# Both branch outputs of a hybrid decoder layer transposed by DMA as 16-bit halves, in place of TensorE transposes

## The reference, cut to what matters

```python
h = rms_norm(x, norm_gain)
aq, ak, av, az, bqkv, bz, bbeta, balpha, gate_a, gate_b = split(h @ w_in)
ya = moba_attention(heads(aq), heads(ak), heads(av)) * silu(az)
bq, bk, bv = split(short_conv(bqkv, conv_w))
g    = -exp(a_log) * softplus(balpha + dt_bias)
beta = sigmoid(bbeta)
o  = gated_delta_rule(heads(bq), heads(bk), heads(bv), g, beta)
yb = rms_norm(o, dn_norm_gain) * silu(heads(bz))
merged = sigmoid(gate_a) * (ya @ w_branch_a) + sigmoid(gate_b) * (yb @ w_branch_b)
x = x + merged @ w_out
return rms_norm(x, final_norm_gain)
```

## Time and profile before

| what | value |
|---|---|
| time, median of 3 runs | 789.8 us |
| the profiled execution's own time | 789.82 us |
| its span | 788.1 us |
| mean granted TensorE clock | 0.997 of 2.4 GHz |
| PE busy | 777.5 us (99%) |
| DVE busy | 550.4 us (70%) |
| ACT busy | 404.6 us (51%) |
| POOL busy | 76.2 us (10%) |
| data moved by DMA | 143.09 MB, mean 182 GB/s |

### The profile page before, as it was taken

One profiled execution on the slowest core, in us unless ns is written; L12 is line 12 of the kernel. 1 busy time (PEld: TensorE's weight loads), 2 busy tenths in 40 slices (PEclk: granted clock), 3 DMA queues, 4 the chain that ended last, 5 costly groups with the idle time before them and its releaser, 6 DMA issues.

```text
span 788.1 us, 12805 instructions
## 1 busy us (share of the span) xinstructions
PE 777.5 (99%) x3651; PEld 642.8 (82%) x3651; DVE 550.4 (70%) x1265; ACT 404.6 (51%) x609; POOL 76.2 (10%) x151
## 2 busy tenths in 40 slices
PE   8999999999999999999999999999999999999996
PEld 7878888888888888888888888888888888888884
DVE  5789659956975796589569847974896466765563
ACT  5765445544554655455455445554554654345440
POOL 5110101010100100110101000001101000001120
PEclk9999999999999999999999999999999999999998
DMA  9946675665656556656756665657555566577652
GB/s 249 254 127 186 184 191 151 183 189 157 186 167 186 152 178 176 184 144 193 193 152 183 176 188 141 197 147 205 145 178 182 176 202 184 180 267 270 184 167 107
DMA packets 181161, 143.09 MB, mean 182 GB/s; under 512 B 11024, under 2 KB 146192, under 8 KB 181008
## 3 DMA queue, kind: packets, MB, share of 16 engines
q1 hardware_dynamic: 180992, 142.52, 62.7%
q10 hardware_dynamic: 144, 0.26, 0.1%
HBM read 140.64 MB, written 2.11 MB: 181 GB/s over the span
## 4 chain that ended last, share of the span: by engine, by line
PE 96%; DVE 2%; issue 1%; DMA 1%; SPq 0%; ACT 0%; POOLq 0%; POOL 0%; DVEq 0%; ACTq 0%
PE pj L551 28%; PE pj L549 28%; PE pj L550 28%; PE dn_ps L601 1%; PE pj L834 1%; PE pj L832 1%; PE pj L833 1%; DMA w_raw<-in_w_in_dram 1%; PE dn_ps L588 1%; PE dn_ps L622 0%; PE dn_ps L627 0%; DVE conv L1212 0%; PE mo_ps L657 0%; PE mo_ps L664 0%; PE dn_ps L602 0%
## 5 line engine op out<-in xcount | busy, mean ns | idle before, releaser
L1083 DVE TENSOR_TENSOR w_lo<-w_raw,w_hi 128x1024 fp32r<-128x1024 f32 x251 | 307.1, 1227 | 139.6 <-ACT w_hi L848 138.4
L549 PE MATMUL pj<-w_hi,xt_hi 128*128 128x512 f32 x860 | 346.2, 403 | 0.4 <-DVE w_lo L1083 0.4
L551 PE MATMUL pj<-w_hi,xt_lo 128*128 128x512 f32 x860 | 336.7, 391 | 0.0
L550 PE MATMUL pj<-w_lo,xt_hi 128*128 128x512 f32 x860 | 335.5, 390 | 0.0
L848 ACT ACTIVATE w_hi<-w_raw 128x1024 fp32r<-128x1024 f32 x251 | 263.4, 1056 | 132.2 <-PE pj L551 122.7
L551 PEld LDWEIGHTS pj<-w_hi,xt_lo 128*128 128x128 f32 x860 | 161.4, 188 | 34.7
L549 PEld LDWEIGHTS pj<-w_hi,xt_hi 128*128 128x128 f32 x860 | 161.7, 188 | 32.5 <-ACT gate L992 1.1
L550 PEld LDWEIGHTS pj<-w_lo,xt_hi 128*128 128x128 f32 x860 | 161.9, 188 | 30.3
L1271 DVE SCALAR_TENSOR_TENSOR xs<-lrep,xs 128x31 f32<-128x31 f32 (+30 forms) x496 | 79.9, 236 | 0.1
L1212 DVE SCALAR_TENSOR_TENSOR conv<-dn_ps,hs,conv 128x255 f32<-128x255 f32 (+2 forms) x72 | 29.4, 472 | 0.0
L484 POOL TENSOR_TENSOR xo<-v,own 128x128 f32<-128x128 f32 x16 | 7.3, 459 | 221.5 <-DVE v L1280 180.9
(11 more groups left out here) (296 smaller groups left out, 702.3 us busy)
## 6 DMA issues: line engine op xcount, KB each, us to landing
w_raw<-in_w_in_dram SPq DMA_DIRECT2D x384, 256.0 KB, 3.1
w_raw<-in_w_out_dram SPq DMA_DIRECT2D x64, 256.0 KB, 3.7
w_raw<-in_w_branch_a_dram SPq DMA_DIRECT2D x32, 256.0 KB, 3.4
w_raw<-in_w_branch_b_dram SPq DMA_DIRECT2D x32, 256.0 KB, 3.4
gate<-in_x_dram SPq DMA_DIRECT2D x8, 256.0 KB, 5.2
gate<-in_x_dram SPq DMA_DIRECT2D x4, 512.0 KB, 7.7
gate<-in_final_norm_gain_dram SPq DMA_DIRECT2D x1, 1024.0 KB, 8.9
out_dram<-gate SPq DMA_DIRECT2D x4, 256.0 KB, 3.6
```

Of the source, the lines that this page charges most:

```text
L549: pe.matmul(bank[:, t, :], hi[:, k, tok], w_hi[:, slot, cs], start=(k == 0), stop=False)
L550: pe.matmul(bank[:, t, :], hi[:, k, tok], w_lo[:, slot, cs], start=False, stop=False)
L551: mm = pe.matmul(bank[:, t, :], lo[:, k, tok], w_hi[:, slot, cs], start=False, stop=(k == kt_all - 1))
L1083: dve.tensor_tensor(w_lo[:, slot, :], w_raw[:, slot, :], w_hi[:, slot, :].bitcast(F32), ALU.subtract).then_inc(lo_ready, 1)
```

## The change

PE no longer transposes `ya` and `yb`. ACT copies each one, seen as 16-bit words, into `halves`, where the low 16 bits of all 256 words of a row (of a partition) stand first and the high 16 bits behind them. SP issues one DMA that transposes the four 128 x 128 tiles of 16-bit words from SBUF to SBUF (`halves` to `halvesT`, 128 KB). ACT then copies `halvesT` to `yT` with the halves put together again, and after it makes `ya_hi` (or `yb_hi`) from `yT` instead of from PSUM. DVE reads `yT` too.

The places: `ya` is laid apart in slot 46, its DMA stands behind the weight DMAs of unit 6 of the next head on SP (J_YA), and it is joined in slot 51 (M_YT). `yb` is laid apart in slot 64 (S_YB), its DMA stands behind those of unit 15 (J_YB), and it is joined in slot 68 (S_YT). There is one `halves`, one `halvesT` and one `yT` for both. In `mo_step` ACT has the same code for `ya` at M_YA and M_YT, and on ACT and DVE the steps of branch A now run on into the next head's iteration, as those of branch B did. The loop over `w_branch_a` on SP is written out, since its seventh and its last unit carry the transposes of the last head.

```diff
+J_YA, J_YB = 6, 15
-S_Y0, S_R1, S_Y1, S_O, S_YT = 55, 57, 59, 61, 66
+S_Y0, S_R1, S_Y1, S_O, S_YB, S_YT = 55, 57, 59, 61, 64, 68
-M_NAT, M_TURN, M_QK, M_EXP, M_PT, M_PV, M_YT = 32, 36, 38, 40, 42, 44, 46
+M_NAT, M_TURN, M_QK, M_EXP, M_PT, M_PV, M_YA, M_YT = 32, 36, 38, 40, 42, 44, 46, 51
+        halves = sb("halves", [P, 2, T * P], U16)
+        halvesT = sb("halvesT", [P, 2 * T, P], U16)
+        yT = sb("yT", [P, T * P])
@@ SP
+            def turn_by_dma(landed):
+                sp.dma_start_transpose(halvesT[:, :, :], halves[:, :, :].rearrange("p e n -> p (e n)")).then_inc(landed, 16)
                     if used is not None:
                         sp.wait_ge(lo_ready, used)
+                    if not first and j == J_YA:
+                        sp.wait_ge(ya_halves, h)
+                    if not first and j == J_YB:
+                        sp.wait_ge(yb_halves, h)
...
+                    if not first and j == J_YA:
+                        turn_by_dma(ya_landed)
+                    if not first and j == J_YB:
+                        turn_by_dma(yb_landed)
...
-            with sp.Fori(0, NC) as c:
+            for c in range(NC):
                 chunk(w_a, c, BU, FIRST_A)
@@ PE
-                    if not first:
-                        pe.wait_ge(yb_lo_ready, h)
-                if s == S_YT:
-                    pe.wait_ge(yb_ready, T * h + T)
-                    pe.wait_ge(ya_lo_ready, h + 1)
-                    for t in range(T):
-                        mm = pe.transpose(C[:, t * P:(t + 1) * P], yb[:, t, :], ident[:, :])
-                    mm.then_inc(ybT_done, 1)
-                if s == M_YT:
-                    pe.wait_ge(ya_ready, T * h + T)
-                    for t in range(T):
-                        mm = pe.transpose(C[:, t * P:(t + 1) * P], ya[:, t, :], ident[:, :])
-                    mm.then_inc(yaT_done, 1)
@@ ACT
+            def halves_of(m):
+                return m.bitcast(U16).rearrange("p (n e) -> p e n", e=2)
+            def turned_back(ready):
+                act.activation(halves_of(yT[:, :]), halvesT[:, :, :].rearrange("p (e t) n -> p e (t n)", e=2), ACT.Copy
+                               ).then_inc(ready, 1)
+                if s == S_YB:
+                    act.wait_ge(yb_ready, T * h + T)
+                    act.wait_ge(ya_landed, 16 * h + 16)
+                    act.activation(halves[:, :, :], halves_of(yb[:, :, :].rearrange("p t n -> p (t n)")), ACT.Copy).then_inc(yb_halves, 1)
                 if s == S_YT:
-                    act.wait_ge(ybT_done, h + 1)
-                    act.activation(yb_hi[:, bass.ds(h, 1), :].rearrange("p a n -> p (a n)"), C[:, 0:SEQ],
+                    act.wait_ge(yb_landed, 16 * h + 16)
+                    act.wait_ge(ya_lo_ready, h + 1)
+                    turned_back(ybT_ready)
+                    act.wait_ge(ybT_ready, h + 1)
+                    act.activation(yb_hi[:, bass.ds(h, 1), :].rearrange("p a n -> p (a n)"), yT[:, :],
                                    ACT.Copy).then_inc(yb_hi_ready, 1)
...
@@ ACT and DVE, iteration
                         dn_step(s + SLOTS, h - 1)
+                        mo_step(s + SLOTS, h - 1)
@@ DVE
-                    dve.tensor_tensor(yb_lo[:, hd, :], C[:, 0:SEQ].rearrange("p (a n) -> p a n", a=1),
+                    dve.tensor_tensor(yb_lo[:, hd, :], yT[:, :].rearrange("p (a n) -> p a n", a=1),
                                       yb_hi[:, hd, :].bitcast(F32), ALU.subtract).then_inc(yb_lo_ready, 1)
...
```

More of the change, by code:

```diff
@@ L10 @@
 F32R = mybir.dt.float32r
+U16 = mybir.dt.uint16
 P = 128
@@ L224, in build @@
             "o_squared", "o_mean", "ro_ready", "yb_ready"))
-        ybT_done, yb_hi_ready, yb_lo_ready = sem("ybT_done"), sem("yb_hi_ready"), sem("yb_lo_ready")
+        yb_hi_ready, yb_lo_ready = sem("yb_hi_ready"), sem("yb_lo_ready")
+        ya_halves, yb_halves, ya_landed, yb_landed = (sem(n) for n in ("ya_halves", "yb_halves", "ya_landed", "yb_landed"))
+        yaT_ready, ybT_ready = sem("yaT_ready"), sem("ybT_ready")
         mo_z_ready, mo_turned, moT_ready, qk_done = (sem(n) for n in (
@@ L231, in build @@
         pt_done, pt_ready, pv_done, ya_ready = sem("pt_done"), sem("pt_ready"), sem("pv_done"), sem("ya_ready")
-        yaT_done, ya_hi_ready, ya_lo_ready = sem("yaT_done"), sem("ya_hi_ready"), sem("ya_lo_ready")
+        ya_hi_ready, ya_lo_ready = sem("ya_hi_ready"), sem("ya_lo_ready")
         sig_ready, a_gated, b_gated, merged = sem("sig_ready"), sem("a_gated"), sem("b_gated"), sem("merged")
@@ L334, in chunk @@
                                      wmat[k * P:(k + 1) * P, bass.ds(col, CH)]).then_inc(w_landed[slot], 16)
-            with sp.Fori(0, NC) as c:
+                    if wmat is w_a and c * units + j == J_YA:
+                        sp.wait_ge(ya_halves, H)
+                        turn_by_dma(ya_landed)
+                    if wmat is w_a and c * units + j == J_YB:
+                        sp.wait_ge(yb_halves, H)
+                        turn_by_dma(yb_landed)
+            for c in range(NC):
                 chunk(w_a, c, BU, FIRST_A)
@@ L983, in mo_step @@
                     act.activation(probT[:, :], C[:, 0:3 * P], ACT.Copy).then_inc(pt_ready, 1)
-                if s == M_YT:
-                    act.wait_ge(yaT_done, h + 1)
-                    act.activation(ya_hi[:, bass.ds(h, 1), :].rearrange("p a n -> p (a n)"), C[:, 0:SEQ],
+                if s == M_YA:
+                    act.wait_ge(ya_ready, T * h + T)
+                    if not first:
+                        act.wait_ge(yb_landed, 16 * h)
+                    act.activation(halves[:, :, :], halves_of(ya[:, :, :].rearrange("p t n -> p (t n)")), ACT.Copy).then_inc(ya_halves, 1)
+                if s == M_YT:
+                    act.wait_ge(ya_landed, 16 * h + 16)
+                    if not first:
+                        act.wait_ge(yb_lo_ready, h)
+                    turned_back(yaT_ready)
+                    act.wait_ge(yaT_ready, h + 1)
+                    act.activation(ya_hi[:, bass.ds(h, 1), :].rearrange("p a n -> p (a n)"), yT[:, :],
                                    ACT.Copy).then_inc(ya_hi_ready, 1)
@@ L1027, in _ @@
                     dn_step(2 * BU * c + 2 * j + SLOTS, H - 1)
+                    mo_step(2 * BU * c + 2 * j + SLOTS, H - 1)
                     tail_split(FIRST_A + BU * c + j + LEAD)
                     dn_step(2 * BU * c + 2 * j + 1 + SLOTS, H - 1)
+                    mo_step(2 * BU * c + 2 * j + 1 + SLOTS, H - 1)
                     n = BU * c + j - 5
@@ L1305, in dn_step @@
                     dve.wait_ge(ro_ready, h + 1)
+                    if not first:
+                        dve.wait_ge(yb_halves, h)
                     r = ro[:, 1, :]
@@ L1336, in mo_step @@
                     if not first:
-                        dve.wait_ge(yaT_done, h)
+                        dve.wait_ge(ya_halves, h)
                     for t in range(T):
@@ L1343, in mo_step @@
                     hd = bass.ds(h, 1)
-                    dve.tensor_tensor(ya_lo[:, hd, :], C[:, 0:SEQ].rearrange("p (a n) -> p a n", a=1),
+                    dve.tensor_tensor(ya_lo[:, hd, :], yT[:, :].rearrange("p (a n) -> p a n", a=1),
                                       ya_hi[:, hd, :].bitcast(F32), ALU.subtract).then_inc(ya_lo_ready, 1)
```

## The result

The changed kernel takes 827.2 us (median of 4 runs, 826.87 to 830.78), the kernel before 790.2 us beside it. The ratio is 1.048 (95% interval 1.046 to 1.049). The forecast of 787.0 us was wrong, and so was the upper end of its range, 810 us.

The account below looks back on a forecast made before the run. PE, busy 99% of the span, was taken to bound the kernel: 3.5 us saved on transposes less 0.7 us lost to late landings gives -2.8, from 789.82 to 787.0 us. The range was 785.8 to 810 us.

Parts of the forecast that it names:

- the sum's form: Whole kernel: loss 8 x (L - 3.9) + 7 x (L - 3.6), positive terms only, against a gain of 3.5 us.
- Rival 2: DMA transpose much slower than a plain DMA: L at 6.2 us, PE waiting at the same two places, 823 us; chance 0.12.
- The gain: PE drops 16 pairs of transposes at 0.22 us each on the chain, 3.5 us in all.
- L: Time from issue to landing of the DMA transpose from halves to halvesT, taken as 3.7 us.
- four tiles one after another: Estimate from the skill's 1309 ns per tile by DMA: 5.2 us of moving alone for one transpose.
- The copies on ACT: Four copies of 512 16-bit words per partition per head, into halves and yT, 0.6 us each.
- the budgets for L: Latest landing before PE waits: L up to 3.9 us for ya, up to 3.6 us for yb.
- Rival 3: ACT's 16-bit copies take 1.3 us each, shrinking the budgets for L; 800.8 us; chance 0.08.
- The loss from late landings: PE's waits when transposes land beyond the budgets for L: 0.7 us in total at L = 3.7.
- rival 1: Transpose lands a little late, PE waits in two places of each head; 791.1 to 808 us, middle 798; chance 0.25.
- its own range: Range of the main forecast alone, L up to 3.87 us: 785.8 to 788.2 us; chance 0.44.
- What would show it: Signs to check: PE idle or not ahead of L630 and L601, iteration about 72.7 us, transpose landing within 4 us.

Follow-up runs that it names:

- e2: The kernel before with one DVE instruction less ahead of its loop (a covered wait for const_made), no transposing DMA; 827.1 us, ratio 1.0466.
- e1: The changed kernel with one tiny DVE instruction more (memset of an unused column) right ahead of the loop over heads; 788.9 us, ratio 0.9985.
- e5: The kernel before without PE's 32 transposes, ya and yb taken untransposed, outputs not the reference's; 786.1 us, ratio 0.9950.
- e4: As e1, but a plain DMA copy of the same 128 KB replaces the transposing DMA, outputs not the reference's; 787.85 us in one run.
- e3: As e1, with the joins later: ya in slot 53 instead of 51, yb in slot 75 instead of 68; 787.2 us, ratio 0.9962.
- e7: The kernel before with 122 tiny DVE memsets spread over the first iteration, ahead of the loop; 807.1 us in one run.

## Why the prediction was wrong, point by point

**The step that failed** is the sum's form: "The question is only what the new path does to PE's own waits", with one gain term and one loss term for the landing. It had no term for where the code stands. I compared the order of the instructions at three places and the durations of all, but not how many instructions stand ahead of DVE's loop. Their number fell from 193 to 192, and that alone is worth 37 us (e2) to 38 us (e1): six turns at which DVE stands still for 5.2 us on average, PE is idle for 4.3, and PE then works at the lower clock. None of the rivals named it. Rival 2's 823 us came near the measured 827 by chance: its mechanism asked for a landing of 6.2 us and waits at L630 and L601, and the landings took 5.0 us at most.

**The gain** was right: 3.5 us forecast, 3.9 measured (e5).

**L**, forecast as 3.7 us, has a median of 3.3 in e1 and 3.9 in the changed kernel. The row that it was taken from, `cum_row` with 3.2 to 4.6, was the right one; e4 shows that a plain copy in the same place lands almost like the transpose. The Trainium skill (Advanced Engine Details and Errata, X-Bar Transpose) has transposing DMAs as fast as regular ones; by that rule, the trace agrees: 3.3 against 3.2 us. The Trainium skill (VectorE: DVE Perf Modes, The three transpose paths) has 1309 ns for one tile by DMA. The estimate by it, four tiles one after another, does not agree: four tiles cost 0.1 us of landing more than the plain copy here.

**The copies on ACT** were taken at 0.6 us each. Laying apart took 0.63, joining 0.79, so the budgets for L were about 0.2 us smaller than worked out, 3.7 and 3.4 us. Rival 3, 1.3 us a copy, falls.

**The loss from late landings** was forecast as 0.7 us and is about 2.8: e1 takes 788.9 us where e5, without any transposition, takes 786.1. The sum was mis-built as well as too small. It took one L for every head, and by it the median of 3.3 us would have cost nothing, since it lies inside both budgets. So it was in six heads: landings of 3.1 to 3.4 us, and PE busy throughout. The loss comes from single landings at the two ends of the program's heads. For the first head's `yb`, 4.7 us, PEld waits 1.7 us at `convs` and PE itself 1.3. For the last head's `ya_lo` PEld waits 1.0 us and PE 0.6, and this wait was missing in my sum. Why the first and the last transposes land later than the twelve between is not shown. The path from a late landing to `convs` is one that rival 1 named, but it had PE wait in two places of each head, and that does not happen. e3 removes 1.8 of the 2.8 us. Rival 1's own arithmetic was also slightly off: its sum at L = 4.1 gives 791.4 us and not 791.1, and in the middle, L = 4.65, 799.6 and not 798. Without the shift in the code the forecast of 787.0 us would have been 1.9 us too low, and its own range (785.8 to 788.2) would have been missed by 0.7 us.

**What would show it** had no sign for a cause outside the new path. "If L is short and PE waits nonetheless, the order on ACT or its 16-bit copies are the cause" would have sent the reader to the wrong engine: L was short, PE waited, and the 28.3 us stand at DVE's L1325. A list of signs should say what follows when a wait appears in a place that nobody watched.

## What to carry to other kernels

Where an engine's list has a hardware loop, count the instructions ahead of it and in it, in the built program, before and after any change. Here a loop of 263 instructions cost nothing at the places 0 and 121 of a piece of 128, 37 to 38 us at the place -1 and 16 us at the place 122. The signs were a stall at the first instruction of a loop with "issue" as the releaser, as many times as the loop turns, and more records on the instruction queue. One harmless instruction ahead of the loop tested it, and from the place -1 it also took the stall away. From the place 122 it would take six more by the pieces of 128; that is an estimate, and no run tried it. And a transfer that must land just in time is better read a few slots later, where the buffers allow it: that gave 1.8 us here at no cost.

## What the runs showed of the hardware

- Code of DVE is loaded in records of 8 KB, and a loop over one piece more made every turn load five of them; a turn then stalls DVE for 2.9 us on average in e7, 5.0 in e2 and 5.2 in the changed kernel. The Trainium skill (Advanced Engine Details and Errata, ISA Cache) gives the engines other than TensorE 32 KB for code, in lines of 256 instructions. Here the records of the queue that grew hold 8 KB, and the measured edges, between -1 and 0 and between 121 and 122, are those of pieces of 128; the measurement decides.
- After PE had been idle for 4 to 4.7 us the granted clock was 0.50 at each of the six turns, in the changed kernel and in e2, while PE worked for 2.9 to 6.0 us. That made some 11 of the 37 us. After 2.0 us of idle time (e7) it fell at two turns of six.
- A 128 KB transpose of 16-bit words in SBUF takes SP 1.20 us to issue and lands 3.3 us after its issue (median in e1), behind two loads of 256 KB; a plain copy of the same bytes takes 0.51 and 3.2 us (e4).
- ACT copies 512 16-bit words per partition with a stride of 4 bytes in 0.63 us when the source is strided (`halves`), and in 0.79 us when the destination is (`yT`).
